# Attention on one NeuronCore: the order of exponentials and copies on ScalarE

## The chip, the core and the metric

The kernel runs on one NeuronCore of a Trainium2 chip. Its engines run each its own list of instructions and meet through semaphores: TensorE (PE: matmuls and transposes; PEld is its weight load), VectorE (DVE), ScalarE (ACT), GpSimd (POOL) and SyncE (SP, which here only issues DMA). The metric is the device time of one execution in microseconds (us), lower is better. Everything is float32.

## What is computed

Two transformer blocks in a row over 512 tokens of width 1024. The change is in the attention of the first block, which has 8 heads of width 64 in 2 groups of keys and values. Each head attends in three ways, and the three results are mixed with gates:

```
s_c = einsum('bqhgd,bnhd->bhgqn', qc, kc) + head_bias(dist_c)     # 31 compressed keys
p_c = masked_softmax(s_c, dist_c >= 0)
o_c = einsum('bhgqn,bnhd->bqhgd', p_c, vc)
...
p_s = masked_softmax(...)      # selected blocks of 64 keys
...
p_w = masked_softmax(s_w, mask_w)      # window
...
return gc[..., 0:1] * o_c + gc[..., 1:2] * o_s + gc[..., 2:3] * o_w
```

With 512 tokens there are 8 blocks of 64 keys and 16 may be chosen, so the selected branch and the window branch (512 wide) are both plain causal attention, over different keys and values.

## The kernel before

The program is a row of stages; `attention()` (from line 1033) is one of them and lies at about 190 to 300 us of the trace. The stage in front of it makes queries and keys; behind it comes `out1`, whose matmuls are those of line 1317.

**Units.** The work is cut into 36 units, numbered u = 0 to 35 in the list `order`. Queries are taken in four tiles of 128, the last tile first (i = 3, 2, 1, 0). Each tile has nine units: first one for the compressed keys of all eight heads (units 0, 9, 18, 27, called compressed units here), then eight for the pairs of heads j = 0 to 3 and, within a pair, the branches b = 0 and 1. A unit of a pair has 128(i+1) keys, so 512, 384, 256 and 128 in the four tiles. The two units of a pair share one output bank.

**Steps of a unit**, each written as a small function, with its engine and line:

- scores, S (PE, L1072): query times keys into PSUM
- maxima, M (DVE, L1140 compressed, L1144 others): adds the bias, writes the scores to SBUF and finds the shift of the softmax
- exponential, E (ACT, L1196 compressed, eight instructions; L1200 others, two instructions)
- turn, T (PE, L1085): transposes the probabilities into PSUM banks 4 and 5, always the same two
- keep, K (ACT, L1207): two copies of the turned probabilities to SBUF
- weigh, W (PE, L1099 compressed, L1104 others): probabilities times values
- and once for a pair: combine (DVE, L1162 to L1166; L1151 to L1156 for a compressed unit), the sum of the branches (POOL, L1186 and L1187), turn_out (PE, L1112), and keep_out, KO (ACT, L1212), which copies the turned output and so frees one of the two output banks.

A number behind the letter is the unit's: K8 is the keep of unit 8.

**What sets the order.** Each engine's order is written out by hand in a loop over u. In round u, PE does S(u), T(u-1), turn_out(u-4), W(u-2). DVE does M(u) and then the combine of u-3. ACT does K(u-1), KO(u-4), E(u); turn_out and KO occur only in rounds where unit u-4 is the second of its pair. The waits are: S(u) for M(u-2); M(u) for S(u); E(u) for M(u); T(u) for E(u) and for K(u-1), since there is one set of banks for turned probabilities; K(u) for T(u); W(u) for K(u). The first W of an output bank also waits until the bank two outputs earlier is empty, which means its KO. Since a compressed unit is one unit and a pair is two, that earlier bank is emptied later than usual, namely in the very round in which it is wanted, for three units: W10 waits for KO8, W19 for KO17, W28 for KO26.

Of the kernel before, what the change touches and what calls it, by code (L numbers as in the profile page):

```python
# [156 lines left out]
def build(nc, A, out, upto=99, dump=None):  # L157
    with ExitStack() as ctx:
# [178 lines left out]
        def load(eng, name, dst, src):  # L337

            eng.dma_start(dst, src).then_inc(sem("ld_" + CHAINS.get(name, (name,))[0]), 16)
            loaded[name] = True  # L340
# [692 lines left out]
        def attention():  # L1033
# [10 lines left out]
            NU = len(order)  # L1044

            def nkeys(u):
                i, j, b = order[u]
                return 8 * i + 7 if j is None else (i + 1) * P
# [7 lines left out]
            def out_place(i, j):  # L1056
                return out_bank(i, j)[:, 264:264 + P]
# [131 lines left out]
            def act(eng, steps):  # L1189
                def exponential(u):  # L1190
                    i, j, b = order[u]
                    n = nkeys(u)
                    eng.wait_ge(read_s, u + 1)
                    if j is None:
                        for h in range(8):
                            last = eng.activation(sc_c[:, h, 0:n], sc_c[:, h, 0:n], ACT.Exp, scale=-1.0, bias=low_c[:, h:h + 1])  # L1196
                    else:
                        for g in range(2):
                            a = sc[u % 2][g][:, 0:n]
                            last = eng.activation(a, a, ACT.Exp, scale=-1.0, bias=low[u % 2][:, g:g + 1])  # L1200
                    last.then_inc(exped, 1)

                def keep(u):
                    n = P if order[u][1] is None else nkeys(u)
                    eng.wait_ge(turned, u + 1)
                    for g in range(2):
                        last = eng.copy(pt[u % 2][g][:, 0:n], ps[4 + g][:, 0:n])  # L1207
                    last.then_inc(kept, 1)

                def keep_out(i, j):  # L1210
                    eng.wait_ge(out_turned, pairs.index((i, j)) + 1)
                    eng.copy(mixT[:, j, i * P:(i + 1) * P], out_place(i, j)).then_inc(out_kept, 1)  # L1212

                eng.wait_ge(*fr("gla_out", 2))
                load(eng, "x_again", xT, A["xT"])
                for u in range(NU + 4):
                    if 1 <= u <= NU:
                        keep(u - 1)
                    if u >= 4 and order[u - 4][2] == 1:
                        keep_out(*order[u - 4][:2])  # L1220
                    if u < NU:
                        exponential(u)

            return dict(pe=pe, dve=dve, act=act, pool=pool)


# [2263 lines left out]
```

## Time and profile before

| | |
|---|---|
| runs, median (lowest to highest) | 1845.45 us (1844.09 to 1849.07), 3 runs |
| profiled execution | 1843.52 us, of which the span of the trace is 1841.7 us |
| PE busy | 1758.2 us, 95% of the span |
| DVE, ACT, POOL busy | 970.1, 492.8, 442.9 us |
| mean granted TensorE clock | 0.989 of full |
| attention, 190 to 300 us | 110 us, PE busy 97.85 us, mean granted clock 0.94 |

"Busy" says for how long an engine had an instruction in it. Idle time of an engine that nobody waits for costs nothing; so the rows that matter are those that say who waited, for whom and for how long. The granted clock is the share of full speed that TensorE was given: 1.00 is 2.4 GHz, 0.50 is 1.2 GHz.

### The profile page before, as it was taken

Reading aid. Unit: us, or ns where it says so; the run is one execution under the profiler, and the core shown is the slowest. Engines: PE = TensorE matmul, PEld = TensorE weight load, DVE = VectorE, ACT = ScalarE, POOL = GpSimd, SP = SyncE. Lnnn points to the kernel's source line nnn. Section 1 sums busy time; section 2 is a strip of 40 time slices with the busy share of each in tenths; the row PEclk is TensorE's granted clock in tenths of the full one; section 3 lists DMA queues with packets and bytes.
Section 4 is the critical chain, followed back from the end, with each engine's and each line's share of the span. In section 5 each row is a group of like instructions: output and inputs, shape, how many; then the busy total and the mean of one; then the engine's idle time right before and its main releaser. Section 6 shows DMA issues by size and latency. Waiting matters only on the chain.

```text
span 1841.7 us, 36243 instructions
## 1 busy us (share of the span) xinstructions
PE 1758.2 (95%) x15550; PEld 1313.6 (71%) x15550; DVE 970.1 (53%) x2010; ACT 492.8 (27%) x1123; POOL 442.9 (24%) x482
## 2 busy tenths in 40 slices
PE   7999998999999999999999978988899999999997
PEld 3446675588888888854455448888867788888886
DVE  4560342343444442232332267666686799999543
ACT  3021563220211100033211554444332322222000
POOL 2150011101101110003000026555453255545100
PEclk9999998999999999999999989999999999999999
DMA  6421101344333343333311200000022222222231
GB/s 233 174 69 48 68 1 46 120 155 146 111 133 115 126 137 121 131 103 126 140 46 58 75 1 4 5 4 5 4 99 69 69 92 92 83 88 82 92 104 57
DMA packets 44759, 158.02 MB, mean 86 GB/s; under 512 B 5113, under 2 KB 7817, under 8 KB 43577
## 3 DMA queue, kind: packets, MB, share of 16 engines
q1 hardware_dynamic: 38304, 132.14, 21.9%
q10 hardware_dynamic: 6296, 23.58, 3.3%
q8 instruction: 123, 2.02, 0.4%
q14 instruction: 36, 0.29, 0.0%
HBM read 150.96 MB, written 6.31 MB: 85 GB/s over the span
## 4 chain that ended last, share of the span: by engine, by line
PE 90%; DVE 5%; ACT 3%; issue 1%; DMA 0%; POOL 0%; SPq 0%; DVEq 0%; POOLq 0%; ACTq 0%
PE psum L367 19%; PE psum L1457 15%; PE psum L1633 15%; PE psum L3099 14%; PE psum L1317 3%; PE psum L2970 3%; PE psum L2397 2%; PE psum L2401 2%; DVE mem L2587 2%; PE psum L694 1%; PE psum L1104 1%; PE psum L1266 1%; PE psum L1085 1%; PE psum L1072 1%; PE psum L2163 1%
## 5 line engine op out<-in xcount | busy, mean ns | idle before, releaser
L367 PE MATMUL psum<-mem 128*128 128x512 f32 (+1 forms) x880 | 350.6, 557 | 12.3 <-DMA mem<-in_units 11.0
L367 PEld LDWEIGHTS psum<-mem 128*128 128x128 f32 x880 | 165.6, 190 | 185.4 <-issue 178.7
L1457 PE MATMUL psum<-mem 128*128 128x256 f32 x1232 | 272.5, 380 | 1.2 <-issue 1.2
L1633 PE MATMUL psum<-mem 128*128 128x256 f32 x1232 | 269.7, 379 | 0.0
L1457 PEld LDWEIGHTS psum<-mem 128*128 128x128 f32 x1232 | 230.9, 189 | 38.8 <-issue 6.3
L1633 PEld LDWEIGHTS psum<-mem 128*128 128x128 f32 x1232 | 231.8, 189 | 35.3 <-issue 2.4
L3099 PE MATMUL psum<-mem 128*128 128x256 f32 x1176 | 254.4, 378 | 0.0
L3099 PEld LDWEIGHTS psum<-mem 128*128 128x128 f32 x1176 | 221.5, 189 | 33.2 <-issue 0.5
L3224 DVE SCALAR_TENSOR_TENSOR mem<-psum,mem 128x441 f32<-128x441 f32 (+2 forms) x352 | 215.5, 681 | 0.0
L2397 PE MATMUL psum<-mem 64*64 64x64 f32 x1920 | 74.9, 223 | 11.8 <-DVE mem L2615 5.3
L1384 POOL TENSOR_TENSOR mem<-mem 128x256 f32<-128x256 f32 x22 | 16.7, 758 | 281.9 <-DVE mem L1592 271.1
L2397 PEld LDWEIGHTS psum<-mem 64*64 64x64 f32 x1920 | 65.8, 137 | 17.7 <-DVE mem L2615 10.5
L2553 POOL TENSOR_TENSOR mem<-mem 128x256 f32<-128x256 f32 x12 | 12.0, 996 | 268.4 <-DVE mem L2570 268.4
L1369 DVE TENSOR_TENSOR mem<-mem 128x512 f32<-128x512 f32 (+1 forms) x44 | 29.4, 669 | 84.6 <-DMA mem<-in_units 51.4
L2401 PE MATMUL psum<-mem 64*64 64x64 f32 x1920 | 71.4, 221 | 2.6 <-issue 2.3
L1369 POOL TENSOR_TENSOR mem<-mem 128x512 f32<-128x512 f32 x27 | 35.3, 1308 | 145.5 <-PE psum L3099 139.7
L2704 ACT COPY mem<-psum 128x256 f32<-128x256 f32 x120 | 45.0, 375 | 90.4 <-PE psum L2397 89.3
L2401 PEld LDWEIGHTS psum<-mem 64*64 64x64 f32 x1920 | 64.5, 136 | 4.6 <-issue 2.8
L2614 DVE COPY_PREDICATED mem<-mem,psum 128x256 f32<-128x256 int32 x96 | 41.0, 427 | 35.6 <-PE psum L2401 35.6
L1317 PE MATMUL psum<-mem 128*128 128x512 f32 x128 | 57.3, 610 | 0.6 <-DVEq L1325 0.6
L427 POOL TENSOR_TENSOR mem<-mem 128x512 f32<-128x512 f32 x12 | 15.2, 1267 | 176.2 <-ACT mem L410 176.1
L3147 ACT ACTIVATE mem<-psum,mem 128x512 f32<-128x512 f32 x44 | 30.3, 688 | 84.8 <-DVE psum L3201 65.7
(391 smaller groups left out, 2433.8 us busy)
## 6 DMA issues: line engine op xcount, KB each, us to landing
mem<-in_units SPq DMA_DIRECT2D x246, 512.0 KB, 3.7
mem<-in_cw ACTq DMA_DIRECT2D x2, 2048.0 KB, 11.6
mem<-in_wn ACTq DMA_DIRECT2D x1, 2048.0 KB, 8.5
bias_tiles<-bias_scratch ACTq DMA_DIRECT2D x1, 2048.0 KB
mem<-bias_tiles ACTq DMA_DIRECT2D x1, 2048.0 KB
mem<-in_xT ACTq DMA_DIRECT2D x1, 2048.0 KB, 9.2
x_scratch<-mem ACTq DMA_DIRECT2D x1, 2048.0 KB, 8.9
mem<-x_scratch ACTq DMA_DIRECT2D x1, 2048.0 KB, 11.0
```

The lines of the kernel that those rows point to most:

```text
L367: last = pe.matmul(dst, w[:, k, :], rhs(k), start=(k == 0), stop=(k == 7))
L1317: last = eng.matmul(ps[m % 4], w[:, k - 8 * part, :], rhs(k), start=(k == 0), stop=(k == ktiles - 1))
L1369: eng.tensor_tensor(to[:, 0][at], w2[at], w2[hi], ALU.add).then_inc(done, 1)
L1457: last = eng.matmul(dst, w[:, k, :], rhs(k), start=start and k == 0, stop=stop and k == 3, skip_group_check=True)
L1633: ins = eng.matmul(dst, w[:, k, :], rhs(k0 + k), start=opens and first and k == 0, stop=closes and last_ and k == k1 - k0 - 1, skip_group_ ...
L2397: each(lambda hp, c, t: eng.matmul(dst(E_[d], hp, t), g[t, hp, 1, :], T[t, hp, :], start=True, stop=True)).then_inc(q["made"], 1)
L2401: each(lambda hp, c, t: eng.matmul(dst(O_[d], hp, t), a[t, hp, :], b_[t, hp, :], start=True, stop=True)).then_inc(q["made"], 1)
L2614: steps.link(eng.copy_predicated(split(T), bc22(kept), heads(O_[d])))
L2704: eng.copy(split(s["Z"]), heads(E_[d])).then_inc(q["kept"], 1)
L2970: last = eng.matmul(dst, w[:, k, :], rhs(k), start=opens and k == 0, stop=closes and k == 3, skip_group_check=True)
L3099: last = eng.matmul(dst, w[:, k, :], rhs(k), start=start and k == 0, stop=stop and k == 3, skip_group_check=True)
L3224: return eng.scalar_tensor_tensor(acc, src, w, acc, ALU.mult, ALU.add)
```

## The change

The body of ACT's loop is put in another order. E(u) now stands at the head of round u instead of at its end, ahead of K(u-1) and KO(u-4). No instruction is added or taken away, and the order on all other engines is the same. Semaphores and their counts are unchanged.

```
                 for u in range(NU + 4):
+                    if u < NU:
+                        exponential(u)
                     if 1 <= u <= NU:
                         keep(u - 1)
                     if u >= 4 and order[u - 4][2] == 1:
                         keep_out(*order[u - 4][:2])
-                    if u < NU:
-                        exponential(u)
```

ACT in the kernel before, where the tile with 512 keys ends and the one with 384 begins. The rows are K8, E9, K9, KO6, E10, K10, E11, K11, KO8, E12, K12.

```order
L1207 COPY mem<-psum 128x512 x2
L1196 ACTIVATE mem<-mem 128x23 x8
L1207 COPY mem<-psum 128x128 x2
L1212 COPY mem<-psum 128x128
L1200 ACTIVATE mem<-mem 128x384 x2
L1207 COPY mem<-psum 128x384 x2
L1200 ACTIVATE mem<-mem 128x384 x2
L1207 COPY mem<-psum 128x384 x2
L1212 COPY mem<-psum 128x128
L1200 ACTIVATE mem<-mem 128x384 x2
L1207 COPY mem<-psum 128x384 x2
```

ACT at the same place in the changed kernel: E9, K8, E10, K9, KO6, E11, K10, E12, K11, KO8, E13.

```order
L1196 ACTIVATE mem<-mem 128x23 x8
L1207 COPY mem<-psum 128x512 x2
L1200 ACTIVATE mem<-mem 128x384 x2
L1207 COPY mem<-psum 128x128 x2
L1212 COPY mem<-psum 128x128
L1200 ACTIVATE mem<-mem 128x384 x2
L1207 COPY mem<-psum 128x384 x2
L1200 ACTIVATE mem<-mem 128x384 x2
L1207 COPY mem<-psum 128x384 x2
L1212 COPY mem<-psum 128x128
L1200 ACTIVATE mem<-mem 128x384 x2
```

The eight small exponentials of compressed unit 9 (L1196) moved in front of K8, each later E in front of the K it followed, and the second L1212, which is KO8, now has E12 in front of it and of K11.

ACT in the kernel before, where the last tile (128 keys) begins. The rows are K25, KO22, E26, K26, E27, K27, KO24, E28.

```order
L1207 COPY mem<-psum 128x256 x2
L1212 COPY mem<-psum 128x128
L1200 ACTIVATE mem<-mem 128x256 x2
L1207 COPY mem<-psum 128x256 x2
L1196 ACTIVATE mem<-mem 128x7 x8
L1207 COPY mem<-psum 128x128 x2
L1212 COPY mem<-psum 128x128
L1200 ACTIVATE mem<-mem 128x128 x2
```

ACT at the same place in the changed kernel: E26, K25, KO22, E27, K26, E28, K27, KO24.

```order
L1200 ACTIVATE mem<-mem 128x256 x2
L1207 COPY mem<-psum 128x256 x2
L1212 COPY mem<-psum 128x128
L1196 ACTIVATE mem<-mem 128x7 x8
L1207 COPY mem<-psum 128x256 x2
L1200 ACTIVATE mem<-mem 128x128 x2
L1207 COPY mem<-psum 128x128 x2
L1212 COPY mem<-psum 128x128
```

E27, eight instructions, moved in front of K26; the pattern is that of the first place with smaller tiles.

## Rows read from the trace of the kernel before

**Rows 1.** Waits of attention, 188 to 300.5 us: who waited for whom, us, times, longest.

```profile
PE psum L1085 <- ACT mem L1196: 4.0, 4, 2.2
PE psum L1104 <- ACT mem L1212: 2.5, 3, 1.1
...
PE psum L1085 <- ACT mem L1200: 2.3, 7, 0.6
```

**Rows 2.** Chain that ended last (start us, us, what), K0 and E1.

```profile
194.81 0.43 ACT mem L1207 x2
195.25 1.24 ACT mem L1200 x2
```

**Rows 3.** Timeline (start, us, engine, line): end of M1, then T1 and T2.

```profile
193.59 0.08 DVE L1144 DVE_READ_ACCUMULATOR2_ANT mem<- 128x1 f32 x1
...
196.53 1.97 PE L1085 MATMUL psum<-mem 128*128 128x128 f32 x8 [0.28 <-ACT mem L1200]
...
200.89 1.10 PE L1085 MATMUL psum<-mem 128*128 128x128 f32 x8 [0.30 <-ACT mem L1200]
```

**Rows 4.** Timeline: S12 on PE and the end of M12 on DVE.

```profile
232.60 0.92 PE L1072 MATMUL psum<-mem 64*128 64x384 f32 x4
...
234.52 0.08 DVE L1144 DVE_READ_ACCUMULATOR2_ANT mem<- 128x1 f32 x1
```

**Rows 5.** Chain: E11, K11, KO8 and W10.

```profile
232.69 1.02 ACT mem L1200 x2
...
234.68 0.86 ACT mem L1207 x2
235.54 0.18 ACT mem L1212
...
235.85 1.52 PE psum L1104 x12
```

**Rows 6.** Chain: S, T and W of one round with 384 keys, on PE alone.

```profile
240.32 0.84 PE psum L1072 x4
241.16 0.81 PE psum L1085 x6
241.97 1.29 PE psum L1104 x12
```

**Rows 7.** Timeline: end of M9.

```profile
225.14 0.08 DVE L1140 DVE_READ_ACCUMULATOR2_ANT mem<- 128x1 f32 x1
```

**Rows 8.** Chain: K8 and E9.

```profile
225.10 1.07 ACT mem L1207 x2
...
226.17 1.65 ACT mem L1196 x8
```

**Rows 9.** Timeline: end of M27.

```profile
277.15 0.08 DVE L1140 DVE_READ_ACCUMULATOR2_ANT mem<- 128x1 f32 x1
```

**Rows 10.** Chain: K26, E27 and T27.

```profile
276.70 0.65 ACT mem L1207 x2
277.35 1.57 ACT mem L1196 x8
...
278.96 0.44 PE psum L1085 x2
```

**Rows 11.** Timeline: S21 on PE and the end of M21 on DVE.

```profile
260.49 0.70 PE L1072 MATMUL psum<-mem 64*128 64x256 f32 x4
...
261.93 0.08 DVE L1144 DVE_READ_ACCUMULATOR2_ANT mem<- 128x1 f32 x1
```

**Rows 12.** Chain: W19, and later an E with 256 keys.

```profile
262.89 1.08 PE psum L1104 x8
...
265.87 0.81 ACT mem L1200 x2
```

**Rows 13.** Stretches (us, PE busy (instructions), granted clock, DMA share, GB/s).

```profile
277.00:280.60 3.60, 2.56 (x24) 1.00 0.02 5
280.60:284.00 3.40, 3.40 (x15) 0.50 0.00 0
```

More of the change, by code:

```diff
@@ L1216, in act @@
                 for u in range(NU + 4):
+                    if u < NU:
+                        exponential(u)
                     if 1 <= u <= NU:
@@ L1220, in act @@
                         keep_out(*order[u - 4][:2])
-                    if u < NU:
-                        exponential(u)
             return dict(pe=pe, dve=dve, act=act, pool=pool)
```

## Prediction

> **What bounds the kernel now.** I read the page first: TensorE (PE) is busy for 95% of the span (the table above). So ACT's order can only matter where PE waits for ACT. Then I read the waits of the attention stage, the only place where the two kernels differ. PE itself waits 4.0 us for L1196 and 2.3 us for L1200 there [rows 1], both the exponentials in front of a turn, T. This 6.3 us of a kernel of 1845 us is what the new order aims at. Last I read the timeline and the chain that ended last round by round, because the waits say where PE stood, and not what will be late next.
>
> The old loop from turn to turn is T(u-1), K(u-1), E(u), T(u): copy and exponential both lie between two turns. In the new one E(u) lies beside T(u-1), and only K(u-1) stands between them, if M(u), the maxima, are ready in time. That condition decides. M(u) needs S(u), and S(u) stands only one step ahead of T(u-1) on PE. If M(u) is late, the new order makes K(u-1), whose input is ready, wait for it, and KO(u-4) behind that.
>
> That ACT does not let a ready copy pass a waiting exponential, or the reverse, is shown at the start. M1 ended at 193.67 [rows 3], yet E1 ran only at 195.25, behind K0 [rows 2]. The Trainium skill, "PSUM — Partial Sum Buffer", section "Engine vs sequencer instructions", says that the queues of ScalarE, VectorE and GpSimdE are strict FIFO. The rule speaks against this change. By it the terms below stand; if a ready copy could pass a waiting exponential, those of the three banks (2.4) and of units 9, 18 and 27 (0.95) would be gone, and the sum of 3.15 would be -0.2.
>
> **The change, place by place.** No instruction is added, so the cost is waits alone. Each term is the difference of two times counted from the same event on PE, so the terms add.
>
> The start. PE waits 0.28 us in front of T1 and 0.30 in front of T2, both for an exponential [rows 3]. E1's input was there at 193.67, so with E1 ahead of K0 both waits go, and PE goes from one block to the next. Term: -0.6.
>
> Tile with 512 keys, six more rounds. PE is not waiting in them, nor should it later: of all units these give PE the most work for the chain to hide behind. Term: 0.
>
> Unit 9, compressed. M9 ends at 225.14 + 0.08 = 225.22 [rows 7]. New: E9 of 1.65 starts then, K8 of 1.07 follows [rows 8], and with some 0.06 for two handovers T9 can start at 228.00. Before it started behind E9, at 226.17 + 1.65 + 0.04 = 227.86. Term: +0.1. The exponential gained nothing, since it started only 0.95 earlier and the copy of 1.07 is now behind it.
>
> W10, the first of the three banks. Before: S12 starts at 232.60, and W10 at 235.85 [rows 4, 5], 3.25 behind it; it waits for KO8. KO8 stood behind K11 alone. Now it stands behind E12 and K11, and E12 needs M12. From the start of S12: M12 ends at 234.60, that is 2.00 later [rows 4]; then E 1.02, K 0.86, KO 0.18, and 0.16 for handovers (0.02 to ACT, 0.13 to 0.14 from KO to W) [rows 5]. W10 starts 4.22 behind S12. Term: 4.22 - 3.25 = +1.0. This is the largest one. PE has nothing else to do there: its next instructions stand behind W10.
>
> W19, the second. Before 262.89 - 260.49 = 2.40 [rows 11, 12]. New: M21 ends 1.52 behind the start of S21 [rows 11], then E 0.81 [rows 12], K 0.65 [rows 10], KO 0.18 and 0.16 [rows 5], together 3.32. Term: +0.9.
>
> W28, the third, with tiles of 128 keys. The same pattern with smaller pieces, and part of it lies in a stretch of half clock. The first two terms were about as long as an E; I take +0.5, with bounds of 0 and 0.9.
>
> Rounds with 384 keys in which PE never waited. A round is 0.84 + 0.81 + 1.29 = 2.94 of PE [rows 6]. The new chain from S(u) to T(u): 2.00 to the end of M [rows 4], 0.02, E 1.02, K 0.86 [rows 5], 0.04, together 3.94. From T(u) on PE to S(u+2) it is T 0.81 and W 1.29, 2.10 [rows 6]. Two rounds then take at least 6.04 instead of 5.88, so each grows by 0.08. Four such rounds: +0.3. In the tile with 256 keys, PE already waited about 0.1 a round, and the new loop is as long as the old to within 0.05: +0.1.
>
> Unit 27, compressed. M27 ends at 277.23 [rows 9]; new E 1.57, K 0.65, 0.06: 279.51. Before T27 at 278.96 [rows 10]. Term: +0.55. Unit 18, with a K of middle size, lies between this and unit 9: +0.3.
>
> Last tile and end. There DVE, POOL and turn_out form the chain; the change leaves it as it is, and the exponentials taken earlier are waited for by nobody. Term: 0, with bounds of -0.9 (one E and one KO at the end) and +0.5.
>
> Sum: -0.6 + 0.1 + 1.0 + 0.9 + 0.5 + 0.3 + 0.1 + 0.55 + 0.3 = +3.15 us. What stands behind attention starts later by that and is otherwise untouched.
>
> **The clock.** PE ran at 1.00 from 277.0 to 280.6, busy 2.56 of 3.60 us with waits around unit 27, and at 0.50 from there to 284.0 [rows 13]. So waits here cost twice: these 3.4 us at half clock held work of 1.7 at full clock, and such a stretch costs up to 1.7, less where PE waits anyway. The new order makes PE's waits longer at W10, W19, unit 27 and W28. I expect about one stretch more of this kind, half hidden: +0.8. Bounds are 0 and four stretches at some 1.4, 5.6. The Trainium skill, "TensorE: Matmul & The Clock Gate", section "HAM oscillation — how this bites in real kernels", has the same effect: gaps between groups of matmuls throttle the clock and the next group starts at half rate. The rows agree in kind.
>
> Forecast: 3.15 + 0.8 = about +4.0. Against the profiled execution (span 1841.7 and 1.8 around it, 1843.5) this is 1847.5. That execution lies 1.9 under the median of the runs, 1845.45; so the forecast for the median is **1849.4 us**. A measurement of this kernel tells about 0.3% from no change, 5.5 us, so most of this case reads as no difference.
>
> **The rivals.**
>
> 1. The change does what it is meant to: maxima come early enough, and PE's waits for exponentials go. Then the 6.3 us of [rows 1] go and the time is 1839.2. For it: at the start two of these waits do go. Against: at unit 9 and unit 27 M ends less than one K ahead of the old start of E, worked out above. It would need M(u) a microsecond earlier.
>
> 2. The two effects cancel or nearly: the start and the end gain 0.6 + 0.9, the banks cost 2.4 but parts of it are caught by slack that my sum does not see. Between -1 and +2, say 1846. For it: single terms are fractions of a us read from one execution. Against: W10 has no slack in the rows, since PE already waits there.
>
> 3. Slower: the clock. Each of the longer waits at W10, W19 and unit 27, and the slow last tile, draws a stretch at 1.2 GHz. With three or four stretches at up to 1.4 the sum is 3.15 + 4.2 to 5.6, so about 1853.5. It decides from two stretches fully paid on: then the total passes 5.5. For it: [rows 13], where 1 us of waiting in front of T27 was enough, while the new waits at W10 would be near 2. Against: PE already waited for L1212 three times in before, up to 1.1 us at once [rows 1], and the mean clock of the stage was still 0.94.
>
> 4. The change does not reach the chip as written: excluded by the order of instructions above.
>
> **How the numbers follow.** The forecast case, +2 to +5.5: 0.57. Rival 1: 0.05, and with it most of the chance of faster. Rival 2: 0.14, all within 0.3%. Rival 3, over +5.5: 0.24. So faster by over 0.3%: 0.04; within: 0.72; slower: 0.24. The range runs from 1843.5 (rival 2's end at -1, and a scatter of 1 in the median) to 1855 (four stretches with the sum, and the same scatter); it leaves out rival 1 and the tail of rival 3.
>
> **What would show it.** In the new profile L1085 on PE should wait for L1207 (K) instead of L1200 and L1196. W10, W19 and W28 should wait longer for L1212 than the 2.5 us in all of before [rows 1], near 4 to 5. T1 and T2 should start earlier by 0.3 and 0.6. Attention should end about 3 to 5 us later. If PE's waits for L1212 don't grow, the bank term is wrong; if rounds with 384 keys stay at 2.94, that small term is. If the time moves by more than 5.5 up with terms as above, stretches at 0.50 should be seen between 230 and 280 us.

## The result, and the profile after

| | before | changed |
|---|---|---|
| median (lowest to highest), 6 runs each | 1847.34 us (1844.09 to 1851.45) | 1861.33 us (1858.06 to 1866.58) |
| profiled execution | 1843.52 us | 1866.58 us |
| span of the trace | 1841.7 us | 1864.8 us |
| mean granted TensorE clock | 0.989 | 0.977 |

The ratio is 1.0084, 95% interval 1.0068 to 1.0100: 14 us slower (1861.33 less 1847.34), where I had forecast 4 and a range that ended at 1855. The profiled execution of the changed kernel is the slowest of its six and that of before lies under all of its six, so the two traces are 23 us apart and show more of the effect than a typical pair does. The six runs of the changed kernel have mean clocks of 0.977 to 0.980, the 29 runs of the kernel before on one of the chips 0.984 to 0.991; among those 29, each 0.001 less of mean clock goes with about 1.2 us more (a line fitted through them). That already points at the clock.

First the waits of the attention stage in the changed kernel, 188 to 322.3 us (who waited for whom, us, times, longest).

```profile
PE psum L1104 <- ACT mem L1212: 4.3, 3, 1.7
PE psum L1085 <- ACT mem L1207: 3.0, 7, 1.1
PE psum L1112 <- POOL mem L1187: 2.4, 2, 2.0
PE psum L1085 <- ACT mem L1196: 2.2, 1, 2.2
```

This is what I had said it would look like: turns wait for copies (L1207) and no longer for L1200 (the 2.2 us for L1196 are the wait of T0), and W for KO (L1212) went from 2.5 us [rows 1] to 4.3. But these waits together are 11.9 us. The corresponding four of before are 4.0, 2.5 and 2.3 [rows 1] and this one, together 11.3:

```profile
PE psum L1112 <- POOL mem L1187: 2.5, 3, 2.0
```

The 20 us that attention grew by are not in PE's waits at all. They are in its busy time. (A slower PE also has less to wait for, so equal sums do not mean that the waits cost nothing; the filled kernels below show what they cost.) The same stage as one stretch of each kernel, from S0 to the first matmul of the next stage, and the part from 272 to 300 us (us, PE busy (instructions), granted clock, DMA share, GB/s). Before:

```profile
190.10:300.40 110.30, 97.86 (x713) 0.94 0.07 25
272.00:300.00 28.00, 21.96 (x152) 0.84 0.00 1
```

Changed:

```profile
191.30:322.20 130.90, 118.23 (x712) 0.76 0.06 21
272.00:300.00 28.00, 27.88 (x133) 0.51 0.00 1
```

The same 712 or 713 instructions kept PE busy for 118.23 us instead of 97.86: 20.4 us more busy and 20.6 us longer. The mean clock fell from 0.94 to 0.76. A mean of 0.76 between 0.50 and 1.00 is 48% of the stage at half clock (1.2 GHz), 63 us of 130.9; 0.94 is 12%, 13 us of 110.3. From 272 to 300 us PE was busy for 27.88 of 28 us, at a mean clock of 0.51. By tiles, from the first S of each to that of the next, the stage grew by 0.6 us (512 keys), 4.8 (384), 8.8 (256) and 6.4 (128); the tile with 256 keys ran at a mean clock of 0.72 and the last at 0.50, where before had 1.00 and 0.81.

Two places on the timeline of PE show where the clock went (start, us, engine, line, [idle before, releaser]). The first is W10:

```profile
234.59 0.92 PE L1072 MATMUL psum<-mem 64*128 64x384 f32 x4
236.12 0.84 PE L1085 MATMUL psum<-mem 128*128 128x128 f32 x6 [0.61 <-ACT mem L1207]
...
238.81 2.79 PE L1104 MATMUL psum<-mem 128*128 128x65 f32 x12 [1.74 <-ACT mem L1212]
241.54 1.65 PE L1072 MATMUL psum<-mem 64*128 64x384 f32 x4
```

S12 is at 234.59 and W10 at 238.81, 4.22 later. I had worked out 4.22; before it was 3.25 [rows 4, 5]. But the twelve matmuls of W10 then take 2.79 us, where they took 1.52 in before [rows 5], and the next S takes 1.65 where a full clock gives 0.92. The wait itself went as summed, and the work behind it ran at half rate. The second place is W19:

```profile
267.46 0.70 PE L1072 MATMUL psum<-mem 64*128 64x256 f32 x4
268.51 0.63 PE L1085 MATMUL psum<-mem 128*128 128x128 f32 x4 [0.35 <-ACT mem L1207]
...
270.77 1.08 PE L1104 MATMUL psum<-mem 128*128 128x65 f32 x8 [1.52 <-ACT mem L1212]
271.77 0.70 PE L1072 MATMUL psum<-mem 64*128 64x256 f32 x4
272.41 0.80 PE L1085 MATMUL psum<-mem 128*128 128x128 f32 x4
```

From S21 to W19 it is 3.31 us (summed: 3.32). The clock fell at about 272.8 and stayed at half until the matmuls of the next stage had run for some us, at 327, so for 54 us. The chain that ended last has no wait in it for 23 us from there on; this is a piece of it (start, us, what):

```profile
282.63 1.16 PE psum L1072 x4
283.79 1.05 PE psum L1085 x4
284.84 1.60 PE psum L1104 x8
286.44 1.16 PE psum L1072 x4
```

One round is 1.16 + 1.05 + 1.60 = 3.81 us of PE at half clock. The same round in before took 2.06 us of PE at full clock (S22 at 263.89 to S23 at 265.95). So at half clock PE itself is the bound in these rounds and ACT's order no longer matters, and in this execution nothing in the stage ended that state.

### The profile page after: what moved, and what is told of

Same layout as the page of the kernel before. It is cut to its first block, busy times and chain, and to the rows that moved or that the text cites. A ratio compares the mean times of both kernels' runs of the same rounds, so it can differ in the third digit from the quotient of the medians.

```text
span 1864.8 us, 36243 instructions
## 1 busy us (share of the span) xinstructions
PE 1778.9 (95%) x15550; PEld 1330.6 (71%) x15550; DVE 971.5 (52%) x2010; ACT 492.0 (26%) x1123; POOL 443.4 (24%) x482
## 4 chain that ended last, share of the span: by engine, by line
PE 89%; DVE 6%; ACT 3%; issue 1%; DMA 0%; POOL 0%; SPq 0%; DVEq 0%; POOLq 0%; ACTq 0%
PE psum L367 18%; PE psum L1457 15%; PE psum L1633 14%; PE psum L3099 14%; PE psum L1317 3%; PE psum L2397 2%; PE psum L2970 2%; PE psum L1104 2%; PE psum L2401 2%; PE psum L1072 2%; DVE mem L2587 2%; PE psum L694 1%; PE psum L1266 1%; PE psum L1085 1%; PE psum L2163 1%
## 5 line engine op out<-in xcount | busy, mean ns | idle before, releaser
L1144 DVE CUSTOM_DVE_ANT_0 mem<-psum,mem 128x512 f32<-128x512 f32 (+3 forms) x64 | 28.9, 489 | 62.6 <-PE psum L1072 62.6
```

## Experiments

The theory, A: the longer waits in front of T11, W10, W19 and W28 take TensorE's clock down, and it then stays down. A2, which `lift` is to test, says why it stays down: with 256 or 128 keys to a unit the work is too thin to bring it back up soon. Rival B: the compressed units, or the small loss in every round. Rival C: chance, since the stretches fall differently in each run. All times are compared with the kernel before on the same chips. In the diffs `ahead` says in which rounds ACT takes E(u) first; in the other rounds E(u) stands last, as before:

```
+                    ahead = <condition>
+                    if u < NU and ahead:
+                        exponential(u)
                     if 1 <= u <= NU:
                         keep(u - 1)
                     if u >= 4 and order[u - 4][2] == 1:
                         keep_out(*order[u - 4][:2])
-                    if u < NU:
+                    if u < NU and not ahead:
                         exponential(u)
```

**The banks undone.** `ahead = u not in (12, 21, 30)`.

> The changed kernel, but in rounds 12, 21 and 30 ACT keeps the order of before (K, KO, E), so that KO8, KO17 and KO26 don't stand behind an E. Theory A (the waits at the three banks take TensorE's clock down, and it then stays down): W10, W19, W28 wait again as in before, 2.5 us in all instead of 4.3; most of the half-clock time in attention goes (68 us in the changed kernel, 17 in before), the time falls from 1861.3 to 1848-1851. Rival B (the compressed units' waits, or the small loss in every round, do it): 2.4 us of structure at most goes, 1857-1860, and the long half-clock stretch stays. Rival C (it is only a matter of chance where a run falls): no clear order, the single runs scatter over 1845-1865.

1852.67 us median, ratio 1.0028 (1.0016 to 1.0040). Two thirds of the loss are gone with three of 36 rounds, though the time is 1.7 over A's range and so is not all the way back. The attention stage of its trace:

```profile
190.60:307.90 117.30, 101.91 (x712) 0.90 0.06 23
```

**The banks alone.** `ahead = u in (12, 21, 30)`.

> The kernel before, but in rounds 12, 21 and 30 ACT takes E first, so KO8, KO17 and KO26 stand behind it. Theory A: this alone brings the long half-clock stretch: 1855-1862, PE waits near 4.3 us for KO. Rival B: only the 2.4 us of structure: 1848-1851, half-clock time in attention near that of before (17 us).

1851.89 us, ratio 1.0033 (1.0006 to 1.0059). Here A's number missed: I had expected 1855 or more, and B's upper end was 1851. Waits for KO were 5.2 us, and the ten single runs lie between 1847.0 and 1869.2. The run at 1869 has a mean clock of 0.973, lower than any run of the changed kernel, so the three rounds alone can bring much half-clock time, but mostly they bring less; the other rounds of the change have a part in it. At W10 the profiled execution shows that a long wait does not bring a stretch each time. W10 waited longer than in the changed kernel and ran at full clock:

```profile
236.67 1.52 PE L1104 MATMUL psum<-mem 128*128 128x65 f32 x12 [2.06 <-ACT mem L1212]
```

**The compressed units undone.** `ahead = u not in (9, 18, 27)`.

> The changed kernel, but in rounds 9, 18 and 27 ACT keeps the order of before, so the eight exponentials of the compressed units don't delay K8, K17 and K26. Theory A: about 1 us less and the long half-clock stretch stays: 1858-1861. Rival B: the stretch goes, 1849-1852.

1858.92 us, ratio 1.0076 (1.0048 to 1.0104), in A's range. The long waits behind the compressed units are not what brings the loss. In this trace too the clock fell behind W19, but it came back in the middle of the tile with 256 keys:

```profile
275.80:286.00 10.20, 10.20 (x46) 0.51 0.00 0
286.20:294.00 7.80, 7.29 (x67) 1.00 0.01 2
```

So the 54 us of the changed kernel are one course that such a stretch can take, and not the only one.

**The clock held by more work.** The whole change, and on PE, in front of W10, W19 and W28:

```
+                    if u in (12, 21, 30):
+                        for _ in range(3):
+                            eng.matmul(ps[2 * ((u - 1) % 2)], ident, zT[:, ZQ, :], start=True, stop=True)
                     if 2 <= u < NU + 2:
                         weigh(u - 2)
```

> The changed kernel with three more matmuls of 128 x 512 on PE in each of rounds 12, 21 and 30, in front of W10, W19 and W28, in time in which PE otherwise waits for KO; their result (in a bank that nobody reads) is not used. ACT's order is that of the change, so every wait of it for maxima stays. Theory A: the clock stays up, half-clock time in attention near 17-25 us, time 1848-1853. Rival B: nothing gained, 1860-1864. If structure, and not the clock, made most of the 14 us, also 1860 or more.

1849.60 us, ratio 1.0016 (1.0001 to 1.0031): 12 us less than the changed kernel, by giving PE more to do, with ACT's order left as in the changed kernel. The same place as above (L1210 is K, L1125 the added matmuls):

```profile
234.26 0.92 PE L1072 MATMUL psum<-mem 64*128 64x384 f32 x4
235.79 0.85 PE L1085 MATMUL psum<-mem 128*128 128x128 f32 x6 [0.61 <-ACT mem L1210]
...
236.59 2.74 PE L1125 MATMUL psum<-mem 128*128 128x512 f32 x6
239.16 1.45 PE L1104 MATMUL psum<-mem 128*128 128x65 f32 x12
```

W10 starts 4.90 behind S12, later even than in the changed kernel, since the added matmuls take 2.6 us and the wait was 1.74. But W10 itself takes 1.45 and not 2.79. This settles the main question: most of the loss is the clock, and not the waits for themselves.

**Filling in both kernels.** A helper puts unused matmuls of 128 x 256 (0.43 us each) where PE waits: before T0, before W10, W19 and W28, and before the last turn_out.

```
+                def idle_work(bank, n):
+                    for _ in range(n):
+                        eng.matmul(bank[:, 0:256], ident, zT[:, ZQ, 0:256], start=True, stop=True)
...
+                        if u == 1:
+                            idle_work(ps[6], 4)
                         turn(u - 1)
                     if u >= 4 and order[u - 4][2] == 1:
+                        idle_work(ps[2 * ((u - 1) % 2)], {39: 4}.get(u, 0))
                         turn_out(*order[u - 4][:2])
                     if 2 <= u < NU + 2:
+                        idle_work(ps[2 * ((u - 1) % 2)], {12: 2, 21: 1, 30: 1}.get(u, 0))
                         weigh(u - 2)
```

> The kernel before, with matmuls of 128 x 256 whose result is not used, placed on PE in time in which it waits: four in front of T0, two in front of W10, one in front of W19 and W28, four in front of the last turn_out. Each is about 0.43 us. Theory A (waits and thin work take the clock down): half-clock time in attention falls from 17 us to under 10, time 1842-1845. Rival (the filling costs as much as it saves): 1847-1849.

1838.39 us, ratio 0.9964 (0.9949 to 0.9980): faster than the kernel before, and 3.6 below what I had expected at the least. The changed kernel's filling has {12: 4, 21: 3, 30: 2}.

> The changed kernel with the same filling, four, three and two in front of W10, W19 and W28 because its waits there are longer. With the clock held up in both, what is left between this and the filled kernel before is the structure alone. Theory A: 3 us (my sum was 3.15) more than the filled kernel before, so 1845-1848. If the structure itself cost more than I summed, it would be 5 us or more over the filled kernel before.

1843.75 us, ratio 0.9994 (0.9983 to 1.0004). This too is below its range, by 1.3. With both kernels filled the change costs 5.4 us, not 14; by the expectation, 5 or more means that the structure (the waits and the longer rounds, without the clock) costs more than I had summed. Their waits, the kernel before filled (L1208 is E, L1204 the compressed E, L1220 KO):

```profile
PE psum L1085 <- ACT mem L1208: 2.3, 6, 0.7
PE psum L1085 <- ACT mem L1204: 2.1, 4, 1.0
PE psum L1104 <- ACT mem L1220: 0.8, 3, 0.3
...
PE psum L1112 <- POOL mem L1195: 0.2, 1, 0.2
```

and the changed kernel filled (L1215 is K):

```profile
PE psum L1085 <- ACT mem L1215: 6.8, 11, 1.6
PE psum L1112 <- POOL mem L1195: 2.1, 4, 1.3
...
PE psum L1085 <- ACT mem L1204: 0.3, 1, 0.3
PE psum L1104 <- ACT mem L1220: 0.2, 1, 0.2
```

5.4 us of waits against 9.4, so 4.0 more; and the filling at the banks is five matmuls longer, 2.1 us, which stand for waits too. Part of what the filled kernel before doesn't wait it spends at half clock (mean 0.92 against 0.97 in the two traces, though over all single runs both have the same median clock, 0.992), so this is an estimate rather than a clean measure of structure: between 4 and 6 us, where my sum had 3.15. The first three tiles can be measured cleanly, since both filled kernels ran them at full clock. From S0 to S27, before filled and then changed filled:

```profile
190.30:274.30 84.00, 80.61 (x599) 1.00 0.09 33
```

```profile
191.30:278.20 86.90, 82.05 (x608) 1.00 0.09 31
```

That is 2.9 us of structure, where my terms for these tiles had 2.1. How much the last tile adds stays open.

**Banks and compressed units undone.** `ahead = u not in (9, 12, 18, 21, 27, 30)`.

> The changed kernel, but with the order of before in the rounds of the banks (12, 21, 30) and of the compressed units (9, 18, 27). What is left of the change by my sum: -0.6 at the start, +0.3 and +0.1 in the middle, so -0.2, and the clock of before. Theory A: 1845-1849. If it is still 3 us or more over before, the small loss in every other round is larger than I summed, or costs clock too.

1852.04 us, ratio 1.0031 (1.0017 to 1.0046). A miss, by 3 us: all my large terms are undone and it is still 7 us slower by the medians. The trace shows a half-clock stretch at W10 although W10 waits 1.10 as in before. A difference stands one step ahead of it: T11 waits 0.61 for K10, in before 0.25 for E11.

**One round.** `ahead = u == 11`, which adds just that.

> The kernel before with one single round changed: in round 11 ACT takes E11 ahead of K10. T11 then waits for K10 until about 0.35 us later than before (0.61 instead of 0.25 in the traces), and 1.1 us of wait for KO8 follows. Theory A: these 0.35 us come just in front of the wait that PE has there anyway, and together they take the clock down; the profile shows a half-clock stretch beginning at 236 to 240 us that the kernel before has not, and the time is 2 to 5 us over before (1847-1850 beside 1845). Rival (every small loss counts only for itself): +0.4, the same as before within the scatter, and no half-clock stretch there.

1849.55 us against 1843.89, ratio 1.0026 (1.0013 to 1.0040), in A's range. Timeline of PE:

```profile
232.72 0.92 PE L1072 MATMUL psum<-mem 64*128 64x384 f32 x4
234.25 0.85 PE L1085 MATMUL psum<-mem 128*128 128x128 f32 x6 [0.61 <-ACT mem L1207]
...
236.30 2.45 PE L1104 MATMUL psum<-mem 128*128 128x65 f32 x12 [1.10 <-ACT mem L1212]
238.68 1.65 PE L1072 MATMUL psum<-mem 64*128 64x384 f32 x4
```

The same stretch, 236 to 246 us, in before and then in this kernel:

```profile
236.00:246.00 10.00, 10.00 (x78) 1.00 0.01 2
```

```profile
236.00:246.00 10.00, 9.70 (x39) 0.53 0.01 2
```

PE did 78 instructions in before in these 10 us, and 39 here. A wait longer by 0.36 us, next to one of 1.1 that was there all along, cost the kernel 5.7 us by the medians (2.4 to 7.4 by the interval). The slowdown is clear of noise, but it is no fixed edge: three of the twelve runs lie at 1843.9 to 1844.8, with clocks of 0.987 to 0.989, like those of before. The traces say the same. Where W10 has no filling in front of it, a half-clock stretch began there in all six traces in which T11 waited 0.61 or 0.62 (changed, `banks_old`, `cmp_old`, `both_old`, this one and `lift`), and in one of the three in which it waited 0.25. That one is `early_new` below, whose trace is of the longest of its twelve runs, with exactly the waits of before at this place:

```profile
235.45 0.88 PE L1085 MATMUL psum<-mem 128*128 128x128 f32 x6 [0.25 <-ACT mem L1200]
...
237.54 1.93 PE L1104 MATMUL psum<-mem 128*128 128x65 f32 x12 [1.10 <-ACT mem L1212]
239.41 1.65 PE L1072 MATMUL psum<-mem 64*128 64x384 f32 x4
```

So the longer wait of T11 makes the stretch more likely; a kernel with the waits of before can have it too.

**Bringing the clock back up.** The whole change, with four unused matmuls of 128 x 256 in each of rounds 22 to 26, in no wait.

> The changed kernel with four unused matmuls of 128 x 256 in each of rounds 22 to 26, in front of W20 to W24, where the changed kernel runs at half clock with PE busy all the time. They are 1.7 us of PE at full clock a round, 8.6 in all, not hidden. Theory A2 (the half clock stays because the work of the tiles with few keys is too thin to lift it, not because PE waits): the half-clock stretch ends within these rounds, half-clock time in attention is 20-35 instead of 68 us, and the time is 1855-1861, no longer than the changed kernel in spite of 8.6 us more work. Rival B2 (a long half-clock stretch, once begun, runs its course): half-clock time 60 or more, time 1870-1878.

1864.64 us, ratio 1.0101 (1.0082 to 1.0120). The time missed A2's range by 3.6, and the half-clock time too: 44 us, against 68 in the changed kernel, where A2 had 20 to 35 and B2 60 or more. The clock came back up at the end of the first of these fillings:

```profile
272.84 3.45 PE L1116 MATMUL psum<-mem 128*128 128x256 f32 x8
276.13 1.00 PE L1104 MATMUL psum<-mem 128*128 128x65 f32 x8
...
278.19 1.89 PE L1116 MATMUL psum<-mem 128*128 128x256 f32 x8
```

Eight instructions take 3.45 at first and 1.89 five us later. Then:

```profile
280.00:296.00 16.00, 15.34 (x115) 1.00 0.00 1
299.00:322.00 23.00, 18.68 (x88) 0.57 0.00 1
```

It held until 296 and fell again in the last tile, behind a wait of 1.65 us for K26 in front of T27. So rival B2, that a long stretch runs its course, is out: the stretch behind W19 lasted some 3.5 us here instead of 54. That thin work is what keeps the clock down is not shown by this. It fits the changed kernel, but in `cmp_old` and `banks_new` the clock came back inside the same tile without any filling, after some 10 and 17 us, and here there is one trace. The fillings outside waits cost at least what they gained.

**The first tile.** `ahead = u <= 8`.

> The kernel before with the new order in rounds 0 to 8 only, the first tile. My sum had -0.6 for the start and 0 for the other rounds. If that holds: 1844-1845, half a us under before. The kernel filled at the start showed T2 waiting 0.70 for K1 in the new order and 0.46 for E2 in the old, which says the start gains nothing: then same as before or up to 0.5 over.

1846.14 us, ratio 1.0008 (0.9993 to 1.0023), which can't be told from no change. The term of -0.6 does not show, and runs that scatter from 1838.4 to 1852.8 could not show it.

**More filling.** The kernel before, filled as above and with {12: 2, 18: 1, 21: 1, 27: 2, 30: 1} in front of W.

> The kernel before with the filling of the filled one and two more unused matmuls in round 27 (the wait of T27 for E27 hides them) and one in round 18. Theory A: the half-clock stretch at unit 27 goes in most runs; 1836-1839. If the last tile is thin whatever stands before it: as the filled kernel before, 1838-1840.

1837.94 us, ratio 0.9970 (0.9958 to 0.9982). And the same with {31: 1, 33: 1, 35: 1, 39: 4} in front of turn_out:

> As the previous one with one more unused matmul of 0.43 us in front of the turn_out of rounds 31, 33 and 35, where PE waits 0.15 to 0.3 us for POOL and the rest lies on the path: +0.2 each, 0.6 in all, if the clock is not touched by it; if it holds the clock up through the last tile, 1 to 3 us less: 1834-1838.

1836.82 us, ratio 0.9967 (0.9954 to 0.9980). Both are in their ranges. All three filled versions of the kernel before lie within 1.6 us of each other and cannot be ranked, so the added matmuls of the last two are not shown to gain anything. Each beats both kernels of this study, with PE doing work that nobody reads. The six runs of the last one lie from 1835.5 to 1839.2, where the kernel before has 1839.8 to 1850.4 in 29 on the same chips.

## Why the prediction was wrong

The waits at W10 and W19, the largest terms, were right, and the sign of the sum too. The size was wrong, and the step that failed is the one under **the clock**: "about one stretch more of this kind, half hidden: +0.8", with a bound of four stretches at 1.4, 5.6. It came to 8 to 10 us of the 14 (14.0 by the medians, less the 4 to 6 of structure; the filled kernel with the whole change lies 17.6 under the changed one by the medians, which includes clock that the kernel before had lost as well). In the trace of the changed kernel the half-clock time of attention was 50 us more, 63 against 13, and attention 20.6 us longer. Chance (rival C) decides where in a run the stretches fall, but it doesn't make the loss: the lowest of the six changed runs, 1858.06, lies over the highest of the six before, 1851.45.

What I got wrong about it is its kind. I took a half-clock stretch for an event of 3.4 us that each long wait may draw once, because the row I read [rows 13] showed such a one. The changed kernel has one of 54 us. The trace of before held a warning that I passed over, a stretch three times as long, from its last units into the next stage:

```profile
294.00:304.50 10.50, 7.36 (x18) 0.51 0.27 100
```

Rival 3 had the cause, with the places, W10 and W19, but priced each place at one short stretch and so ended at 1853.5. "It decides from two stretches fully paid on" did not hold either: one round with 0.36 us more wait cost 5.7 by the medians.

Point by point:

- **W10, +1.0; W19, +0.9.** Measured 4.22 and 3.31 from S, against 4.22 and 3.32 worked out. Right.
- **W28, +0.5.** From S30 to W28 it is 2.05 in before and 2.71 in the changed kernel, +0.66, but both lie in part or wholly at half clock; at full clock no trace shows it.
- **Unit 9, +0.1.** From S9 (223.03 before, 224.82 changed) to T9 4.83 and 5.07, so +0.24.
- **Unit 27, +0.55; unit 18, +0.3.** In the filled kernels T27 waits 1.65 instead of 1.04, +0.6, and T18 1.05 instead of 0.61, +0.4.
- **Rounds with 384 keys, 6.04 for two.** In the changed kernel two such rounds are 6.23 with one turn_out of 0.11, so 6.12. The sign was right, the term half again as large.
- **T11.** Missing from the sum. I reckoned W10 from S12 and so left out that T11 ahead of it waits 0.36 longer. It changes no start of W10, and for that reason looked free; it made the stretch at W10 more likely.
- **Start, -0.6.** Not visible in the time. In the changed kernel S0 to T2 is 11.19 us against 10.75, as the half clock there lasted longer; in the filled pair it is 9.53 against 9.88, so -0.35. Removing both waits exposed a new one: T2 waited 0.70 for K1, whose turn had come behind E2.
- **Last tile, 0.** Wrong by its own bound of +0.5: the tile grew by 6.4 us, of which the terms for unit 27 and W28 cover about 1, since at half clock PE takes the place of the chain through DVE and POOL in most of it. The tile with 256 keys grew even more, 8.8.
- **The order of ACT's queue.** No copy overtook a waiting exponential: KO8 came behind E12 and K11 to within 0.01 us of the sum made that way. So the trace agrees with what the prediction cites from the Trainium skill, "PSUM — Partial Sum Buffer", section "Engine vs sequencer instructions": the queue of ScalarE is strict FIFO.

What would show it was named rightly (L1207 in place of L1200 and L1196, and "near 4 to 5" for L1212, which measured 4.3). But attention ended 20.6 us later and not 3 to 5, and the sentence that was to catch the clock looked between 230 and 280 us, while most of it lay behind 280.

What stays open: how much of the 14 us is structure. The filled pair says 5.4 by medians, its waits 4.0, my terms with the corrections above about 4. And what decides in a given run whether a wait starts a stretch and how long it lasts, since the three banks alone gave runs from 1847 to 1869, and the stretches that began in the tile with 256 keys lasted 10, 17 and 54 us.

## What to carry to other kernels

Where TensorE is the bound and its work is thin, sum the waits not only one by one but by how close they stand: a third of a us more beside a wait of one us cost 5.7 us here, since it made ten us at half clock more likely. When a trace grows in busy time with the same number of instructions, look at the granted clock before looking for a new wait. One trace of each kernel is not enough for this, as where the clock falls differs between executions of the same kernel. And a wait that cannot be removed can be filled with unused matmuls: it gained 6 to 7 us here (0.3%), without any reordering.

## What the runs showed of the hardware

PE can be busy almost without a gap and stay at half clock for 29 us: from 272.8 to 302.0 us of the changed kernel it was busy for 29.08 of 29.20 us at 0.50, in units of small matmuls (128 x 128 turned, 128 x 65 weighed), and the whole stretch lasted 54 us. With four unused matmuls of 128 x 256 in between (`lift`) the clock was back at 1.00 within 4 us. In the changed kernel it came back only with the matmuls of the next stage, and in `cmp_old` by itself after 10 us, so its length differs between executions. Unused matmuls in the place of the waits kept the clock up at W10 and W19 in the traces of `warm` and of the filled changed kernel, with the waits in front of T11 and T18 as long as without them.
